# First stage of a hybrid encoder layer: early constants on their own signal, first weights in two halves, x scaled two tiles ahead

## The reference, cut to what matters

```
h = rms_norm(x, norm1_g)                  # x: 768 x 2048
proj = h @ w_in                           # w_in: 2048 x 4960
q_lat, kv_lat, k_rope, qkv, z, a_f, a_b, b_f, b_b = split_cols(proj, SPLITS)
q  = rms_norm(q_lat, q_a_norm_g) @ w_q_b  # q_lat: 512 columns
kv = rms_norm(kv_lat, kv_a_norm_g) @ w_kv_b
```

## Time and profile before

| | |
|---|---|
| median of three runs | 3532.57 us (3531.45 to 3532.7) |
| the profiled execution | 3532.9 us |
| its span, first to last instruction | 3531.1 us |
| first stage, until attention's first matmul | 360.7 us |
| mean granted TensorE clock | 0.971 of full |

### The profile page before, as it was taken

One profiled execution on the slowest core, in us unless ns is written; L12 is line 12 of the kernel. 1 busy time (PEld: TensorE's weight loads), 2 busy tenths in 40 slices (PEclk: granted clock), 3 DMA queues, 4 the chain that ended last, 5 costly groups with the idle time before them and its releaser, 6 DMA issues. The chain is left out here.

```text
span 3531.1 us, 28727 instructions
## 1 busy us (share of the span) xinstructions
PE 3322.6 (94%) x11412; PEld 1763.5 (50%) x11412; DVE 921.9 (26%) x1558; ACT 474.8 (13%) x1235; POOL 259.6 (7%) x328
## 2 busy tenths in 40 slices
PE   5899899899999999988799996999999999999998
PEld 3454444456776766757544553333333333333333
DVE  1100345323654655647400231000000000000000
ACT  2210244212113122132100100000000000000000
POOL 0000111001201202102000000000000000000000
PEclk9999999999999999999899997999999999999999
DMA  4110100022011111030131138888888989888984
GB/s 153 54 64 18 59 25 24 28 84 60 13 54 60 42 49 42 19 128 25 64 126 48 72 143 306 296 323 312 318 316 316 315 321 322 314 316 322 316 312 147
DMA packets 161463, 558.35 MB, mean 158 GB/s; under 512 B 9599, under 2 KB 42199, under 8 KB 138711
## 3 DMA queue, kind: packets, MB, share of 16 engines
q1 hardware_dynamic: 157271, 531.84, 41.7%
q0 software_dynamic: 4096, 25.17, 3.2%
HBM read 523.07 MB, written 33.91 MB: 158 GB/s over the span
## 5 line engine op out<-in xcount | busy, mean ns | idle before, releaser
L2084 PE MATMUL psum<-xT,xeT 128*96 128x512 f32 x1040 | 453.5, 594 | 2.1 <-ACT h L2135 1.4
L2084 PE MATMUL psum<-wbuf,xeT 128*96 128x512 f32 x1008 | 437.6, 592 | 0.0
L1127 PE MATMUL psum<-xT,wbuf 128*128 128x512 f32 x736 | 342.4, 600 | 6.5 <-DVE pre L1470 6.5
L1776 PE MATMUL psum<-wbuf,xT 128*128 128x512 f32 x768 | 336.4, 600 | 1.0 <-PEq L1058 1.0
L2084 PEld LDWEIGHTS psum<-xT,xeT 128*96 128x96 f32 x1040 | 170.0, 164 | 279.5 <-issue 278.6
L2084 PEld LDWEIGHTS psum<-wbuf,xeT 128*96 128x96 f32 x1008 | 164.3, 163 | 268.3 <-issue 268.3
L438 PE MATMUL psum<-wbuf,xT 128*128 128x512 f32 (+1 forms) x704 | 279.9, 557 | 0.0
L1776 PEld LDWEIGHTS psum<-wbuf,xT 128*128 128x128 f32 x768 | 147.5, 193 | 184.9 <-issue 184.9
L2102 PE MATMUL psum<-wbuf,hT 128*96 128x512 f32 x528 | 229.3, 592 | 0.7 <-ACT hT L2130 0.7
L2160 DVE COPY hT<-psum 128x384 f32<-128x384 f32 x16 | 8.9, 557 | 822.6 <-PE psum L2066 822.6
L2102 PE MATMUL psum<-xT,hT 128*96 128x512 f32 x496 | 215.5, 592 | 0.7 <-DVE hT L2160 0.7
(11 more groups left out here) (264 smaller groups left out, 2875.8 us busy)
## 6 DMA issues: line engine op xcount, KB each, us to landing
xT<-in_w_up SPq DMA_DIRECT2D x47, 2048.0 KB, 9.1
wbuf<-in_w_gate SPq DMA_DIRECT2D x46, 2048.0 KB, 7.2
wbuf<-in_w_down SPq DMA_DIRECT2D x33, 2048.0 KB, 9.5
xT<-in_w_down SPq DMA_DIRECT2D x31, 2048.0 KB, 8.1
xT<-in_w_gate SPq DMA_DIRECT2D x18, 2048.0 KB, 7.2
wbuf<-in_w_up SPq DMA_DIRECT2D x17, 2048.0 KB, 11.2
wbuf<-in_w_in SPq DMA_DIRECT2D x12, 2048.0 KB, 8.7
wbuf<-in_w_o SPq DMA_DIRECT2D x6, 4096.0 KB, 13.8
```

The lines of the kernel that those rows point to most:

```text
L1127: last = nc.tensor.matmul(ps[:, b, 0:SS_], wg[:, m % 2, d, h * P:(h + 1) * P], k.xT[:, d, SP_:T], start=(d == 0), stop=(d == KD - 1))
L1776: last = nc.tensor.matmul(ps[:, u % 3, :], mixT[:, q, t * P:(t + 1) * P], wo[:, j % 2, q, :], start=(q == 0), stop=(q == 2 * H - 1))
L2084: last = nc.tensor.matmul(ps[0:CT, 2 * (u // 4) + half, :], xeT[:, q, :], m[:, kk, 512 * half:512 * half + 512], start=(q == 0), stop=(q = ...
```

## The change

- SP issues x0 first, then `square` and `n1g`, which count on a semaphore of their own, `s_first`.
- The first weights go as two transfers of 2048 KB, blocks 0 to 7 on the new `s_w0` and blocks 8 to 15 on `s_w[0]`, with x1 between them. x2 is issued behind them, ahead of the nine other constants.
- VectorE waits at its start for `s_first` alone. It waits for the other nine constants at t = 1, ahead of `store_latent 0`.
- ScalarE scales x0 and x1, and then x(t+2) ahead of `latent t`.
- PE does the first half of projection 0 (blocks 0 to 7), then transposes x1, then does the second half.
- Two semaphores are given up: the signal of eps uses `s_vec`, that of the convolution taps uses `s_gp`.

```
             def _(sp):
-                sp.dma_start(k.square[:], a["square"][:, 0:5 * P]).then_inc(s_const, 16)
-                sp.dma_start(n1g[:], a["norm1_g"].rearrange("o (p k) -> p (o k)", k=KD)).then_inc(s_const, 16)
...
                 load_x(0)
+                sp.dma_start(k.square[:], a["square"][:, 0:5 * P]).then_inc(s_first, 16)
+                sp.dma_start(n1g[:], a["norm1_g"].rearrange("o (p k) -> p (o k)", k=KD)).then_inc(s_first, 16)
+
+                w_first = a["w_in"][0].rearrange("(p k) n -> p k n", k=KD)[:, :, 0:QL]
+                sp.dma_start(wb[0][:, 0:KD // 2, :], w_first[:, 0:KD // 2, :]).then_inc(s_w0, 16)
                 load_x(1)
-                load_w(0)
+                sp.dma_start(wb[0][:, KD // 2:KD, :], w_first[:, KD // 2:KD, :]).then_inc(s_w[0], 16)
+                load_x(2)
...
-                for t in range(2, NT):
+                for t in range(3, NT):
                     load_x(t)
...
-            NCONST = 16 * 11
+            NCONST = 16 * 9
...
-                act.wait_ge(s_eps, 1)
+                act.wait_ge(s_vec, 1)
...
                 scale_x(0)
+                scale_x(1)
                 for t in range(NT):
-                    if t + 1 < NT:
-                        scale_x(t + 1)
+                    if t + 2 < NT:
+                        scale_x(t + 2)
                     latent(t, QL)
...
-                nc.vector.memset(eps_sb[:], EPS).then_inc(s_eps, 1)
-                dve.wait_ge(s_const, NCONST)
+                st.done(nc.vector.memset(eps_sb[:], EPS))
+                dve.wait_ge(s_first, 32)
...
                     if t + 1 < NT:
                         store_x(t + 1)
+                    if t == 1:
+                        dve.wait_ge(s_const, NCONST)
                     if t:
                         store_latent(t - 1)
...
-                dve.wait_ge(s_cv, 1)
-                nc.vector.tensor_copy(convT[:], ps[:, 5, 0:120]).then_inc(s_cv, 1)
+                dve.wait_ge(s_gp, 3)
+                st.done(nc.vector.tensor_copy(convT[:], ps[:, 5, 0:120]))
...
-                pe.wait_ge(s_const, 16 * 2)
+                pe.wait_ge(s_first, 32)
...
-                def project(u):
+                def project(u, lo=0, hi=KD):
...
-                    if t == 0:
+                    if u == 0 and lo == 0:
+                        pe.wait_ge(s_w0, 16)
+                    elif t == 0:
                         pe.wait_ge(s_w[g % 2], 16 * ((g // 2) + 1) + (16 if g % 2 else 0))
...
-                    for d in range(KD):
+                    for d in range(lo, hi):
...
-                    last.then_inc(s_acc, 1)
+                    if hi == KD:
+                        last.then_inc(s_acc, 1)
...
                 transpose_x(0)
-                for t in range(NT):
+                project(0, 0, KD // 2)
+                transpose_x(1)
+                project(0, KD // 2, KD)
+                for t in range(1, NT):
                     if t + 1 < NT:
                         transpose_x(t + 1)
                     project(t)
```

More of the change, by code:

```diff
@@ L212, in latents @@
         s_w = [sem("w_loaded0"), sem("w_loaded1")]
+        s_first = sem("transpose_constants_loaded")
+        s_w0 = sem("first_weight_half_loaded")
         s_const = sem("constants_loaded")
@@ L223, in latents @@
         s_z = sem("z_gated")
-        s_eps = sem("eps_set")
         s_act = sem("scalar_step")
@@ L229, in latents @@
         s_gp = sem("gate_tensor")
-        s_cv = sem("conv_taps")
         s_rows = sem("rows_stored")
@@ L477, in _ @@
                 pe.wait_ge(s_const, NCONST)
-                nc.tensor.transpose(ps[:, 5, 0:120], convr[:], k.ident[0:120, 0:120]).then_inc(s_cv, 1)
+                nc.tensor.transpose(ps[:, 5, 0:120], convr[:], k.ident[0:120, 0:120]).then_inc(s_gp, 1)
                 for u in range(2 * NT + 3, 4 * NT - 2):
```

## The result

The changed kernel takes 3482.32 us in the median of four runs (3479.99 to 3489.16); the kernel before takes 3532.01 (3530.23 to 3532.7, four runs). The ratio is 0.9861, with a 95% interval of 0.9845 to 0.9876. It is 49.7 us faster. I had forecast 37.2 (3495.3, range 3492.0 to 3499.5): the direction was right, and the gain was a third larger than the sum.

The account below looks back on a forecast made before the run. PE, busy 94% of the span, bounds the kernel, so only its idling can be won: 18.2 us to projection 1 and 19.1 in rounds 1 to 3, 37.3 in all, taking 3532.57 to 3495.3 us (range 3492.0 to 3499.5).

Parts of the forecast that it names:

- the part on the clock: First stage, PE: transposes take the same at either clock; the low clock costs only 0.24 us of projection 1.
- the 3.47 us: First stage, PE: time from the start of a tile's transposes to the next projection's start, within a round of 17.68 us.
- the head: Beginning of the first stage: x0 lands at 7.15, projection 1 starts at 37.55 where it was 55.77, 18.2 us won.
- half clock in the first half: Rival, projection 0: the first transposes don't raise the clock, so 16 records run at twice their 0.43 us; 3501.7, 3%.
- The later stages: The four stages behind the first: they move as a whole, as long as before.
- the bounds that I named: Whole kernel: x0's landing +0.8 and -1.6, slow start 0.5, x1's slack 2.1 and 1 more, run spread 1.3; 3492.5 to 3498.
- the 6 us gaps: First stage, PE: some 6 us of idling ahead of the transposes of x2 to x5, awaiting ScalarE's scaling, would vanish.
- the cover of the nine constants: First stage, VectorE: the constants land at 31 at the latest, needed at about 51.8; cost 0, with 20 us of cover.
- the halves did not land together: Rival, first weights: transfers share the engines, the first half lands at 22.1, projection 0 starts 5.75 us late; 3501.0, 5%.
- the head did move: Rival, first stage's beginning: something unseen holds projection 0 at 31.3, only the four gaps' 25.7 us are won; 3506.9, 2.5%.
- the scaling was ahead: Rival, ScalarE: x(t+2) comes too late, rounds keep 24 us, gain is 11.7 us or less; 3521 to 3532, 3%.
- the constants were in time: Rival, VectorE: the nine constants come late and PE stands at projection 3's tile, 1 us per us beyond 51.8; 3542, 1.5%.

Follow-up runs that it names:

- the warm-up matmuls: Changed kernel plus six 128x512 matmuls of a constant, results unread, on PE from about 2 us while it waits for x0: median 3482.07 us.
- The filled gaps: Kernel before plus six 128x512 matmuls, results unread, in PE's idle time ahead of the transposes of each of x2 to x5: median 3521.99 us.
- the second profile: The changed kernel profiled again, with nothing altered: first stage 313.1 us.
- the constants alone: Kernel before with only x0 issued first and `square` and `n1g` early on their own signal; weights whole, scaling one ahead: median 3520.69 us.

## Why the prediction missed, by its own steps

**The step that failed** is the sentence in the part on the clock, "Transposes take the same at either level (3.68 and 3.65)", and with it the 3.47 us that every round and the head were given. I took the 3.65 of x0's transposes for the upper clock since the profile has 1.00 in that stretch:

```profile
13.60:17.40 3.80, 3.65 (x16) 1.00 1.05 386
```

The records of the clock begin with its first change, at 32.4 us in that trace, and the views show 1.00 for what lies ahead. Both numbers were the lower clock: behind the warm-up matmuls x0's transposes took 2.04. At the upper one the 16 transposes take 1.97 us and are followed by the projection after 1.81. From x1 to x5 that is five times 1.66 us = 8.3 us that the sum lacked. The sixth, x0's, stays at the lower clock. The filled gaps show it without any other edit: a round there is 22.4 us (52.91 to 75.27) where it was 24.

**The head.** x0 landed just before 5.78, near the bound that I had from a lone transfer, 5.55, and not at my choice, 7.15 (x1 and x2 came 1.8 us early too, at 15.0 and 23.0); the first half started at 15.04, 1.3 early. It then took 9.26 and not 7.4: the clock rose only at 19.7. In the second profile it rose at 13.3, the half took 7.10 and the stage 313.1. What sets the moment of the rise is not shown. My rival "half clock in the first half" was partly real, at 1.9 of its 6.4 us. The sum to projection 1: -1.3 + 1.9 - 1.66 - 1.66 = -2.8, and 34.78 is 37.55 less that. Three rounds add 5.0: together the stage's 7.8.

**The later stages**, which I let move as a whole, are the other term: 5.3 us in this pair of profiles, 3.7 between the means of three and five (3170.0 and 3166.3 for all that lies behind the first stage). That they were longer or shorter with the clock and not with the work was in reach, since the page had a mean clock of 0.971 on gaps that nobody had to touch. My 1.3 us for the spread between runs was too small as well: more runs of the kernel before lie between 3525.31 and 3539.08. And the bounds that I named don't come to 3492.5 to 3498: added up they give 3491.9 to 3500.5, which leaves the 3482.3 outside all the same.

**What held.** The order of the transfers, the wait for the last constant and its removal, the 6 us gaps and their end, the cover of the nine constants (no wait of VectorE for them), the latent and scaling inside a round, the weights of the later groups: all as written. Of the rivals, the halves did not land together, the head did move, the scaling was ahead, and the constants were in time. The Trainium skill's sentence on transposes (TensorE: Matmul & The Clock Gate, Part 4: PE-mode transpose), that full clock does not engage for them, is not borne out. With matmuls ahead they ran at full clock (1.97 and 2.07), and in the second profile of the changed kernel the rise came at 13.3, when PE had done nothing but x0's transposes from 10.60 on. It can come late: with the constants alone x0's and x1's, close together, both took 3.65 to 3.68, and the rise came at 18.9, still ahead of the first projection (20.35).

## What to carry to other kernels

A gap costs more than its length where the engine's clock falls in it: here 6.1 us of idling ahead of each tile cost 8 us, as the transposes behind it ran at half the clock. Before writing that an operation takes the same at either clock, find a row of it behind work and one behind idling; a clock shown as 1.00 ahead of its first recorded change is no measurement. And when idle time moves in one stage, expect later stages with gaps to move by some us for the clock alone, and take several profiles before giving them a cause.

## What the runs showed of the hardware that I had not expected

- 16 float32 transposes of 128x128: 3.65 to 3.68 us at the lower clock, 1.97 at the upper.
- The core begins at the lower clock: with PE's first work at 10.5, the rise came at 19.7, 13.3, 18.8, 19.7 and 19.1 in five profiles of the changed kernel; with matmuls from 2.04 on, at 4.9.
- Two stages of unchanged code took 1385.2 to 1397.9 us in sixteen profiles, on one line with their time at 0.50.
- Filling four gaps with matmuls whose results nobody reads made the kernel before 8.0 us faster in the stage (6.7 of it in the rounds with the gaps) and 9.5 in the median (3531.48 to 3521.99).
